# Hybrid encoder layer on one core: stick-breaking attention with rounded passes and an output added chunk by chunk, and the mixing product's second part by token tiles

## Chip, core and metric

The kernel runs on one core of a Trainium2 chip. The metric is the device time of one execution in microseconds; the time before is the median of three runs.

The engines are named as in the profile: TensorE is PE (its weight loads PEld), VectorE is DVE, ScalarE is ACT, GpSimd is POOL, SyncE is SP. SP only issues DMA here.

## What is computed

One layer (DEPTH is 1) on x of 1024 tokens by 1024 features, all in float32. A mixing sub-layer is followed by an MLP, each between two RMS norms. The mixing sub-layer has three groups that share one input projection: stick-breaking attention (4 heads of 64), a gated linear recurrence of width 512, and sliding-window attention. Their outputs are normed by group, concatenated and projected by `w_out`.

```python
u = rms_norm(h, g_pre_mix[l])
proj = jnp.einsum('bsd,de->bse', u, w_in[l])
# stick-breaking: A[t,s] = beta_ts * prod_{s<j<t}(1-beta_tj), s<t only
z = jnp.einsum('bhqd,bhkd->bhqk', qi, kf).astype(jnp.float32) * scale
log_beta = jax.nn.log_sigmoid(z)
log_1m = jnp.where(before, jax.nn.log_sigmoid(-z), 0.0)
tail = lax.cumsum(log_1m, axis=3, reverse=True) - log_1m
w = jnp.where(before, jnp.exp(log_beta + tail), 0.0)
out = jnp.einsum('bhqk,bhkd->bhqd', w.astype(vf.dtype), vf)
...
mixed = jnp.concatenate([rms_norm(o_a, ga), rms_norm(o_b, gb), rms_norm(o_c, gc)], axis=-1)
y = jnp.einsum('bse,ed->bsd', mixed, w_out[l])
h = h + rms_norm(y, g_post_mix[l])
u = rms_norm(h, g_pre_mlp[l])
f = jnp.square(jax.nn.relu(jnp.einsum('bsd,df->bsf', u, w_ff_in[l])))
y = jnp.einsum('bsf,fd->bsd', f, w_ff_out[l])
h = h + rms_norm(y, g_post_mlp[l])
```

## The kernel before

The order of each engine's work is written out by hand, and engines meet only at semaphores. A semaphore wait holds up all that is queued behind it on the same engine.

**Rounded passes.** A product of two float32 operands is done as three passes in the format fp32r: each operand is split into a rounded part (`hi`, by ScalarE) and a rest (`lo`, by VectorE), and `three_passes` multiplies hi by hi, hi by lo and lo by hi (lines 648, 650, 652). A plain float32 matmul, as the attention uses it, shows as two records in the trace and streams its columns four times.

**Stick-breaking.** 24 steps (the list `SB`): for each pair of heads (2) and each half of the queries (2), the key blocks of 128 from the last to the first, a chain of 4 or 8 steps. Keys lie on partitions, queries on columns, and the two heads side by side. The first steps of a chain are on the diagonal and have 128, 256, 384 and then 512 columns; all later ones have 512. The widths of a chain of the second half are 128, 256, 384 and five times 512. For a step s:

- TensorE makes the scores (`scores`, line 832) into PSUM banks 0 and 1 or 2 and 3, by the parity of s
- VectorE writes minus their absolute value (`minus_abs`, line 1663), ScalarE does Exp and Ln of it (lines 1233, 1234), VectorE makes the log terms `sb_l` (line 1687), and GpSimd masks the diagonal block
- VectorE adds the carry of the chain so far to the scores in PSUM (line 1697), TensorE adds the triangle product (`exponents`, line 864), and ScalarE takes the Exp: the weights (`weights_exp`, line 1213)
- TensorE sums the log terms over the block by a matrix of minus ones into two banks (`carry`, line 877), which ScalarE copies out (line 1243)
- TensorE multiplies the weights by v, accumulating over the chain (`weighted`, line 892)

TensorE's order in step s is scores(s+1), one part of the fill, exponents(s), carry(s), weighted(s-1), the other part of the fill. The fill (`FILL`) is the recurrent group's part of the output product: from step 4 on a unit of three passes ahead of the triangle, and in even steps two more behind the product with v. Four units make a bank, so 10 of its 16 banks are done in the stage, and VectorE evicts one in every second step (`recurrent_row`, line 1672). The other six follow the stage.

**Mixing product, second part.** The stick-breaking and window groups, 16 units (eight token tiles by two column halves g = 2, 3) of 12 passes. Each unit fills two banks out of a ring of four, and VectorE scales each by the group's norm and adds it to y (line 1754). All tiles of g = 2 come first, then all of g = 3, so a token tile is whole only in the second half. Then, per tile: its squares (ScalarE, line 1050), a root on VectorE of four tiny instructions (lines 1471 to 1465), the gain pass `y_gained` on GpSimd (line 639), the residual (VectorE, line 1733), h stored to DRAM, the squares of h, another root, and the scaled copy for the MLP (`normed`, line 1292).

**MLP.** Stages of seven Strassen products (P1, P2, P6, P5, P7, P3, P4) of 48 passes each. Before P1 the h of tiles 0 to 3 is transposed on TensorE (`turn_hidden_inputs(0)`, line 971) and copied to `ut` by ScalarE and VectorE in turn (lines 1300, 1774); before P2 that of tiles 4 to 7. The operands of each half product are rounded by `round_operands` (lines 1347, 1351) and `rest_operands` (lines 1798, 1805). `block_sum` makes the Strassen sums: S1 to S4 of the activations, T1 to T4 of the weights; T1 needs `wq12` and `wq11`, T2 needs `wq22`.

Of the kernel before, what the change touches and what calls it, by code (L numbers as in the profile page):

```python
# [16 lines left out]
F32 = mybir.dt.float32  # L17
# [66 lines left out]
def encoder_layer(nc, x, g_pre_mix, w_in, conv_w, conv_b, lru_wa, lru_ba, lru_wx, lru_bx,  # L84
# [5 lines left out]
    with ExitStack() as ctx:  # L90
# [16 lines left out]
        def sem(name):  # L107
# [12 lines left out]
        sb_carry = at("sb_carry", [P, 2, BANK], X_AT + 32 * K)  # L120
        neg_tri = at("neg_tri", [P, P], X_AT + 36 * K)
        neg_ones = at("neg_ones", [P, P], X_AT + 36 * K + 512)
# [10 lines left out]
        ut = at("ut", [P, 2, KD, BANK], ACT_AT + 32 * K)  # L133
        h_back = at("h_back", [P, TOK, D], ACT_AT + 32 * K)
# [6 lines left out]
        wq22 = at("wq22", [P, 4, BANK], X_AT + 16 * K)  # L141
        w_sum = at("w_sum", [P, 4, BANK], X_AT + 24 * K)
# [11 lines left out]
        y_gained = at("y_gained", [P, TOK, D], X_AT)  # L154
        out_gained = at("out_gained", [P, TOK, D], X_AT)
# [72 lines left out]
        carry_ready, carry_copied, carry_added = (  # L228
            sem("carry_ready"), sem("carry_copied"), sem("carry_added"))
        expo_ready, w_raw, w_masked, pv_done, o_copied = (  # L230
            sem("expo_ready"), sem("w_raw"), sem("w_masked"),
            sem("pv_done"), sem("o_copied"))
# [8 lines left out]
            [sem(f"h_stored{i}") for i in range(2)])  # L241
# [37 lines left out]
        TILE_SETS = ((0, 1), (2, 3), (4, 5), (6, 7))  # L279
        N_SETS = len(TILE_SETS)  # L280

# [132 lines left out]

        IN_SUMS = ("T2", "S2", "T3", "S3", "S4", "T4", "T1")
        SUMS = (IN_SUMS, ("S1", *IN_SUMS))

        def sum_count(s, name):

            if name == "T1":  # L420
                s -= 1
            if s < 0:
                return 2
            ahead = 2 + sum(len(SUMS[r % 2]) for r in range(s))
            return ahead + SUMS[s % 2].index(name) + 1
# [5 lines left out]
        def _(sp):  # L431
# [88 lines left out]
            sp.wait_ge(carry_added, adds(len(SB) - 1))  # L520
            sp.dma_start(wq11[:, :, :], block_of(0, 0, 0)).then_inc(wq_loaded[0], 16)
            for i in range(TOK):
                sp.wait_ge(h_ready, i + 1)
                sp.dma_start(h_dram[P * i:P * (i + 1), :], y[:, i, :]).then_inc(h_stored[i // 4], 16)
                if i == 3:
                    sp.dma_start(wq21[:, :, :], block_of(0, 1, 0)).then_inc(wq_loaded[2], 16)
                if i == 7:
                    sp.dma_start(wq12[:, :, :], block_of(0, 0, 1)).then_inc(wq_loaded[1], 16)
                    sp.dma_start(wq22[:, :, :], block_of(0, 1, 1)).then_inc(wq_loaded[3], 16)
# [11 lines left out]

            for half in range(2):
                sp.wait_ge(h_stored[half], 16 * 4)
            sp.wait_ge(a_lo_ready, halves(STAGES - 2, P4))
            sp.dma_start(h_back[:, :, :], h_dram.rearrange("(i p) d -> p i d", p=P))\
                .then_inc(h_loaded, 16)
# [9 lines left out]
        def _(pool):  # L556
# [48 lines left out]
            pool.wait_ge(v_turned, 2)  # L605
            after(nc.gpsimd.memset(neg_ones[:, :], -1.0))

# [29 lines left out]
            for i in range(TOK - 1):  # L637
                pool.wait_ge(y_added, banks_out(3) + 2 * (i + 1))
                nc.gpsimd.tensor_tensor(y_gained[:, i, :], y[:, i, :], rs_row[:, :], ALU.mult)\
                    .then_inc(y_gain_done, 1)  # L640
# [4 lines left out]
        def _(pe):  # L645
# [253 lines left out]
            def recurrent_out(n, ks=range(OUT_K)):  # L899
# [11 lines left out]
                elif n < N_EARLY + 4:  # L911
# [3 lines left out]
                    if bank_out(n) == 4:  # L915
                        pe.wait_ge(o_copied, 4)
# [1077 lines left out]
```

## Time and profile before

| | us |
|---|---|
| median of 3 runs (1160.93 to 1162.46) | 1162.07 |
| profiled execution | 1161.97 |
| its span | 1160.2 |
| TensorE busy | 1082.9 (93%) |
| VectorE busy | 808.4 (70%) |
| ScalarE busy | 573.5 (49%) |
| GpSimd busy | 76.1 (7%) |

How to read it: times in rows are microseconds from the start of the span. A row of the timeline has its start, its duration, the engine, the line of the kernel, the operation, what it writes and reads, and in brackets how long the engine had been idle and what ended that. The end of a matmul is modelled, so neighbouring matmuls overlap in the records. PEclk is the clock granted to TensorE as a share of its full 2.4 GHz: 1.00 is that level, 0.50 the 1.2 GHz one.

### The profile page before, as it was taken

The numbers are of one execution on the slowest core, as the hardware profiler recorded it, in microseconds if no ns is written. First come the engines' busy times: TensorE is split into PE (matmuls) and PEld (weight loads), VectorE is DVE, ScalarE is ACT, GpSimd is POOL, SyncE is SP. The second block draws the span as 40 slices with busy tenths as digits, with TensorE's granted clock in tenths as the row PEclk, the third lists the DMA queues.
The fourth block names the chain that finished last, engine by engine and source line by source line (L and its number), as shares of the span: only waits on it lengthen the run. The fifth ranks groups of instructions, "written<-read, shape, count | busy, mean of one in ns | idle before, by whom it ended". The sixth has DMA issues, their size and how long they took to land.

```text
span 1160.2 us, 12115 instructions
## 1 busy us (share of the span) xinstructions
PE 1082.9 (93%) x4844; PEld 845.5 (73%) x4844; DVE 808.4 (70%) x767; ACT 573.5 (49%) x705; POOL 76.1 (7%) x69
## 2 busy tenths in 40 slices
PE   6999999987899999838999999999999999999993
PEld 5877777876535458737888888878888878888782
DVE  2536657655454545777778777789876799867998
ACT  6313533357464640376665546653456543466353
POOL 0004113201101000400000000000000000000000
PEclk9999999978899999978999999999999999999997
DMA  7211112110000023060130310301303003016003
GB/s 220 78 45 37 37 37 73 36 38 1 1 1 1 20 102 114 37 236 1 37 109 1 109 37 21 125 1 37 109 1 114 31 19 127 1 43 248 1 1 145
DMA packets 44624, 70.44 MB, mean 61 GB/s; under 512 B 10228, under 2 KB 19736, under 8 KB 44568
## 3 DMA queue, kind: packets, MB, share of 16 engines
q1 hardware_dynamic: 43528, 69.66, 17.7%
q8 instruction: 39, 0.64, 0.2%
q10 hardware_dynamic: 1040, 0.00, 0.1%
q14 instruction: 17, 0.14, 0.0%
HBM read 61.27 MB, written 8.39 MB: 60 GB/s over the span
## 4 chain that ended last, share of the span: by engine, by line
PE 84%; DVE 8%; ACT 4%; issue 2%; DMA 1%; DVEq 0%; ACTq 0%
PE ps L648 25%; PE ps L652 25%; PE ps L650 25%; PE ps L864 2%; PE ps L724 1%; PE ps L877 1%; PE ps L787 1%; PE ps L892 1%; PE ps L832 1%; DVE sb_e L1663 1%; ACT sb_e L1233 1%; DVE out_gained L1888 1%; DMA g_pre_mix_c<-in_g_pre_mix 1%; ACT sb_w L1213 1%; DVE ps L1697 1%
## 5 line engine op out<-in xcount | busy, mean ns | idle before, releaser
L648 PE MATMUL ps<-a_op,b_op 128*128 128x512 f32 x448 | 175.9, 393 | 5.4 <-DVE b_op L1805 4.5
L648 PE MATMUL ps<-b_op,a_op 128*128 128x512 f32 x448 | 174.6, 390 | 2.7 <-issue 2.7
L650 PE MATMUL ps<-a_op,b_op 128*128 128x512 f32 x448 | 175.6, 392 | 0.0
L652 PE MATMUL ps<-a_op,b_op 128*128 128x512 f32 x448 | 175.4, 392 | 0.0
L652 PE MATMUL ps<-b_op,a_op 128*128 128x512 f32 x448 | 174.3, 389 | 0.0
L650 PE MATMUL ps<-b_op,a_op 128*128 128x512 f32 x448 | 174.3, 389 | 0.0
L648 PE MATMUL ps<-act_hi,w_hi 128*128 128x512 f32 x288 | 115.0, 399 | 3.2 <-DVE w_lo L1455 3.2
L1805 DVE TENSOR_TENSOR b_op<-wq,b_op 128x1024 fp32r<-128x1024 f32 x96 | 116.9, 1218 | 0.0
L1347 ACT CAST a_op<-f 128x1024 fp32r<-128x1024 f32 x56 | 58.8, 1049 | 116.0 <-PE ps L652 75.7
L652 PE MATMUL ps<-act_hi,w_lo 128*128 128x512 f32 x288 | 112.8, 392 | 0.0
L650 PE MATMUL ps<-act_lo,w_hi 128*128 128x512 f32 x288 | 112.6, 391 | 0.0
L648 PEld LDWEIGHTS ps<-a_op,b_op 128*128 128x128 f32 x448 | 84.9, 189 | 23.8 <-issue 6.2
L1798 DVE TENSOR_TENSOR a_op<-f,a_op 128x1024 fp32r<-128x1024 f32 x56 | 68.4, 1222 | 47.6 <-ACT a_op L1347 47.6
L1351 ACT CAST b_op<-wq 128x1024 fp32r<-128x1024 f32 x96 | 100.7, 1049 | 0.0
L648 PEld LDWEIGHTS ps<-b_op,a_op 128*128 128x128 f32 x448 | 84.1, 188 | 21.4 <-issue 4.1
L652 PEld LDWEIGHTS ps<-a_op,b_op 128*128 128x128 f32 x448 | 84.9, 190 | 17.8
L650 PEld LDWEIGHTS ps<-a_op,b_op 128*128 128x128 f32 x448 | 84.8, 189 | 17.7
L652 PEld LDWEIGHTS ps<-b_op,a_op 128*128 128x128 f32 x448 | 84.1, 188 | 17.5
L650 PEld LDWEIGHTS ps<-b_op,a_op 128*128 128x128 f32 x448 | 84.1, 188 | 17.4
L1347 ACT CAST a_op<-ut 128x1024 fp32r<-128x1024 f32 x32 | 33.7, 1052 | 76.0 <-PE ps L652 75.4
L648 PEld LDWEIGHTS ps<-act_hi,w_hi 128*128 128x128 f32 x288 | 54.4, 189 | 16.5 <-issue 5.5
L1040 ACT CAST w_hi<-stage 128x1024 fp32r<-128x1024 f32 x26 | 26.1, 1048 | 77.2 <-PE ps L652 72.0
(190 smaller groups left out, 1759.5 us busy)
## 6 DMA issues: line engine op xcount, KB each, us to landing
wq<-in_w_ff_in SPq DMA_DIRECT2D x16, 1024.0 KB, 5.3
wq<-in_w_ff_out SPq DMA_DIRECT2D x16, 1024.0 KB, 5.1
stage<-in_w_in SPq DMA_DIRECT2D x18, 512.0 KB, 4.7
y<-in_x SPq DMA_DIRECT2D x4, 1024.0 KB, 10.0
stage<-in_w_out SPq DMA_DIRECT2D x8, 512.0 KB, 3.7
h_spill<-y SPq DMA_DIRECT2D x8, 512.0 KB, 3.0
h_back<-h_spill SPq DMA_DIRECT2D x1, 4096.0 KB, 15.5
out<-y SPq DMA_DIRECT2D x8, 512.0 KB, 2.7
```

Of the source, the lines that this page charges most:

```text
L648: nc.tensor.matmul(dst, stat[0], mov[0], start=first, stop=False, skip_group_check=chained)
L650: nc.tensor.matmul(dst, stat[0], mov[1], start=False, stop=False, skip_group_check=chained)
L652: return nc.tensor.matmul(dst, stat[1], mov[0], start=False, stop=last, skip_group_check=chained)
L724: mm = nc.tensor.matmul(ps[:, 4 + 2 * m + half, :], gate_w[:, m, c, :], work[:, 0, BANK * half:BANK * (half + 1)], start=True, stop=True)
L787: mm = nc.tensor.matmul(ps[CHUNK * e:CHUNK * (e + 1), b + i // 4, P * (i % 4) + off:P * (i % 4 + 1)], qt[rows, CHUNK * c:CHUNK * (c + 1)], ...
L832: mm = nc.tensor.matmul(ps[:, 2 * (s % 2) + a, c0:], sk_t[p][rows, P * j:P * (j + 1)], sq_t[p][rows, BANK * half + c0:BANK * (half + 1)], ...
L864: mm = nc.tensor.matmul(ps[:, 2 * (s % 2) + a, c0:], neg_tri[:, :], sb_l[:, s % 2, a, c0:], start=False, stop=True, skip_group_check=True)
L1040: nc.scalar.copy(w_hi[:, slot, 1024 * s:1024 * (s + 1)], stage[:, s, :])\
L1347: nc.scalar.copy(a_op[:, half % A_SLOTS, 0], src).then_inc(a_hi_ready, 1)
L1351: nc.scalar.copy(b_op[:, (half + 3) % B_SLOTS, 0], src).then_inc(b_hi_ready, 1)
L1798: nc.vector.tensor_tensor(slot[:, 1], a_source(s, i, kk), slot[:, 0].bitcast(F32), ALU.subtract)\
L1805: nc.vector.tensor_tensor(slot[:, 1], src, slot[:, 0].bitcast(F32), ALU.subtract).then_inc(b_lo_ready, 1)
```

## The change

In the stick-breaking stage the log terms are split into `sb_hi` and `sb_lo`, and the triangle product and the sum over a block are each done in two rounded passes with tables that are exact in the rounded format. The sums of both heads go to one bank, each head's to its 64 partitions (`ones_r`). The carry is no longer added to the scores: the weights of a block are multiplied by v without it, into a bank of its own, and `add_output` multiplies the result by Exp of the carry (`sb_rest`) and adds it to the output so far.

In the mixing product's second part the units go by token tile (`OUT_ORDER`): the first two tiles of g = 2, the same two of g = 3, then both halves of each further tile. Norms are split in smaller sets and spread between the units, the first four transposes stand ahead of the last unit, T1 and T2 ahead of the operands of P2, and buffers and loads of the MLP's weights move to fit.

```diff
             def exponents(s):
                 c0 = SB[s][3]
-                masked(pe, s, log_raw, log_masked)
-                if adds(s):
-                    pe.wait_ge(carry_added, adds(s))
+                pe.wait_ge(l_lo_ready, s + 1)
                 for a in range(2):
-                    mm = nc.tensor.matmul(ps[:, 2 * (s % 2) + a, c0:], neg_tri[:, :],
-                                          sb_l[:, s % 2, a, c0:], start=False, stop=True,
-                                          skip_group_check=True)
+                    bank = ps[:, 2 * (s % 2) + a, c0:]
+                    nc.tensor.matmul(bank, tri_r[:, :], sb_hi[:, s % 2, a, c0:], start=False,
+                                     stop=False, skip_group_check=True)
+                    mm = nc.tensor.matmul(bank, tri_r[:, :], sb_lo[:, s % 2, a, c0:],
+                                          start=False, stop=True, skip_group_check=True)
                 mm.then_inc(expo_ready, 1)
...
             def carry(s):
...
-                    mm = nc.tensor.matmul(ps[:, 6 + a, c0:], neg_ones[:, :],
-                                          sb_l[:, s % 2, a, c0:], start=first_of_chain(s),
-                                          stop=True, skip_group_check=True)
+                    nc.tensor.matmul(ps[:, 6, c0:], ones_r[:, a, :], sb_hi[:, s % 2, a, c0:],
+                                     start=first_of_chain(s) and a == 0, stop=False,
+                                     skip_group_check=True)
+                    mm = nc.tensor.matmul(ps[:, 6, c0:], ones_r[:, a, :], sb_lo[:, s % 2, a, c0:],
+                                          start=False, stop=a == 1, skip_group_check=True)
...
+            for e, (s, g) in enumerate(OUT_ORDER):
+                n = 2 * TOK + 2 * e
...
+                if s == 0:
+                    pe.wait_ge(w_lo_ready, 2 * (N_IN + g + 1))
...
+                if e == len(OUT_ORDER) - 2:
+                    turn_hidden_inputs(0, range(4))
+            turn_hidden_inputs(0, range(4, KD))
...
+            act.wait_ge(tables_ready, 2)
+            nc.scalar.copy(tri_r[:, :], neg_tri[:, :]).then_inc(tables_rounded, 1)
+            nc.scalar.copy(ones_r[:, :, :], pair_ones[:, :, :]).then_inc(tables_rounded, 1)
             for s in range(len(SB)):
...
                 if s:
                     weights_exp(s - 1)
+                masked(act, s, log_raw, log_masked)
+                nc.scalar.copy(sb_hi[:, s % 2, :, c0:], sb_l[:, s % 2, :, c0:])\
+                    .then_inc(l_hi_ready, 1)
                 if not first_of_chain(s):
...
-                    nc.scalar.copy(sb_carry[:, :, c1:], ps[:, 6:8, c1:]).then_inc(carry_copied, 1)
+                    if s >= 2:
+                        act.wait_ge(o_added, s - 1)
+                    nc.scalar.activation(sb_rest[:, s % 2, c1:], ps[:, 6, c1:], ACT.Exp)\
+                        .then_inc(rest_ready, 1)
...
+            def add_output(s):
...
+                dve.wait_ge(pv_done, s + 1)
...
+                nc.vector.tensor_tensor(sb_part[:, c1:], part[:, c1:], sb_rest[:, s % 2, c1:],
+                                        ALU.mult).then_inc(part_ready, 1)
+                n_parts[0] += 1
+                dve.wait_ge(part_ready, n_parts[0])
+                nc.vector.tensor_tensor(total[:, c1:], total[:, c1:], sb_part[:, c1:], ALU.add)\
+                    .then_inc(o_added, 1)
...
-                    nc.vector.tensor_tensor(z, z, sb_carry[:, :, c1:], ALU.add)\
-                        .then_inc(carry_added, 1)
+                if s >= 2:
+                    add_output(s - 2)
                 for n in range(early(s - 1) if s else 0, early(s)):
                     recurrent_row(n)
                 if s + 1 < len(SB):
                     minus_abs(s + 1)
+                rest_log(s)
...
+            for s in range(len(SB) - 2, len(SB)):
+                add_output(s)
             left = list(range(early(len(SB) - 1), 2 * TOK))
...
+            mix_rows(0)
+            split_lo(N_IN + 3, (N_IN + 3) % 2)
+            for j in range(3):
+                for e in range(4 * j + 1, 4 * j + 5):
+                    if e == 12:
+                        mlp_root(0)
+                    mix_rows(e)
+                mix_tiles(j)
+            mix_rows(13)
+            mix_rows(14)
+            turned(0, (1, 3))
+            mix_rows(15)
+            turned(0, (5, 7))
+            rest_operands(0, [0])
+            mix_tiles(3)
+            rest_operands(0, [1])
+            mix_tiles(4)
+            mlp_root(1)
+            mlp_root(2)
+            block_sum(0, "T1")
+            mlp_root(3)
+            block_sum(0, "T2")
+            rest_operands(1, [0])
+            turned(1, (1, 3, 5, 7))
+            rest_operands(1, [1])
             block_sum(0, "S1")
-            block_sum(0, "T1")
```

ScalarE's order changes likewise: squares and roots are spread between the tiles, `round_operands(1, [0])` stands ahead of the squares of tile 7, and the load of `wq12` follows the store of tile 7's h. The load of `h_back` at the end is cut in two.

## Rows read from the trace of the kernel before

**Rows 1.** Table of stretches: start:end, length, busy time of each engine, granted clock, DMA.
```profile
279.00:430.00 151.00, 138.09 (x507) 69.26 (x508) 77.75 (x88) 83.44 (x107) 15.09 (x33) 0.97 0.05 16
560.00:1119.00 559.00, 556.28 (x2452) 459.54 (x2451) 449.80 (x339) 299.90 (x282) 0.00 (x0) 1.00 0.18 61
291.00:294.00 3.00, 1.41 (x10) 0.50 (x8) 2.01 (x2) 2.11 (x3) 0.76 (x2) 1.00 0.00 0
294.00:297.00 3.00, 2.67 (x3) 1.18 (x4) 0.50 (x2) 0.83 (x2) 0.00 (x0) 0.54 0.03 5
```

**Rows 2.** Timeline, steps 12 to 13 and 20 to 22.
```profile
350.35 0.42 DVE L1663 TENSOR_SCALAR sb_e<-ps 128x256 uint32<-128x256 uint32 x1 [0.68 <-PE ps L832]
354.78 0.69 DVE L1663 TENSOR_SCALAR sb_e<-ps 128x512 uint32<-128x512 uint32 x1 [1.99 <-PE ps L832]
...
393.03 1.23 DVE L1663 TENSOR_SCALAR sb_e<-ps 128x1024 uint32<-128x1024 uint32 x1 [1.12 <-PE ps L832]
400.26 1.21 DVE L1663 TENSOR_SCALAR sb_e<-ps 128x1024 uint32<-128x1024 uint32 x1
401.27 1.88 PE L864 MATMUL ps<-sb_l,neg_tri 128*128 128x512 f32 x4
404.79 1.08 PE L892 MATMUL ps<-sb_w,vtok 128*64 128x512 f32 x4
408.56 1.22 DVE L1663 TENSOR_SCALAR sb_e<-ps 128x1024 uint32<-128x1024 uint32 x1 [1.31 <-PE ps L832]
```

**Rows 3.** Groups by line and form, 279 to 430 us: busy, mean ns, idle before.
```profile
L1233 ACT ACTIVATE sb_e<-sb_e 128x1024 f32<-128x1024 f32 x12 | 12.7, 1057 | 33.2 <-DVE sb_e L1663 33.2
L1213 ACT ACTIVATE sb_w<-ps 128x1024 f32<-128x1024 f32 x12 | 12.1, 1011 | 9.1 <-PE ps L864 9.1
```

**Rows 4.** Timeline, mixing product's second part and MLP start.
```profile
449.90 0.75 DVE L1754 SCALAR_TENSOR_TENSOR y<-ps,rstd,y 128x512 f32<-128x512 f32 x1
...
506.21 5.19 PE L971 MATMUL ps<-ident,y 128*128 128x128 f32 x32 [14.91 <-ACT y L1292]
515.87 0.55 PE L648 MATMUL ps<-a_op,b_op 128*128 128x512 f32 x1 [4.46 <-DVE b_op L1805]
528.46 1.91 PE L971 MATMUL ps<-ident,y 128*128 128x128 f32 x16
536.62 0.77 PE L648 MATMUL ps<-a_op,b_op 128*128 128x512 f32 x1 [0.94 <-DVE ut L1774]
```

**Rows 5.** The page's costliest groups: operand rest on VectorE, rounding copy on ScalarE.
```profile
L1805 DVE TENSOR_TENSOR b_op<-wq,b_op 128x1024 fp32r<-128x1024 f32 x96 | 116.9, 1218 | 0.0
L1347 ACT CAST a_op<-f 128x1024 fp32r<-128x1024 f32 x56 | 58.8, 1049 | 116.0 <-PE ps L652 75.7
```

**Rows 6.** Timeline, end of the stick-breaking stage.
```profile
415.79 1.22 DVE L1663 TENSOR_SCALAR sb_e<-ps 128x1024 uint32<-128x1024 uint32 x1
423.64 0.75 DVE L1672 TENSOR_SCALAR y_early<-ps,rstd 128x512 f32<-128x512 f32 x1 [0.94 <-PE ps L652]
427.45 0.50 PE L648 MATMUL ps<-w_hi,f_hi 128*128 128x512 f32 x1
```

**Rows 7.** Timeline, start of the stick-breaking stage.
```profile
284.90 0.83 ACT L1233 ACTIVATE sb_e<-sb_e 128x768 f32<-128x768 f32 x1
294.09 0.41 DVE L1663 TENSOR_SCALAR sb_e<-ps 128x256 uint32<-128x256 uint32 x1
```

**Rows 8.** The page's DMA issues: a weight block, KB, us to landing.
```profile
wq<-in_w_ff_in SPq DMA_DIRECT2D x16, 1024.0 KB, 5.3
```

**Rows 9.** Timeline: a root's instruction beside a GpSimd pass, and without.
```profile
479.43 2.42 POOL L639 TENSOR_TENSOR y_gained<-y,rs_row 128x1024 f32<-128x1024 f32 x1 [0.32 <-DVE y L1754]
479.46 2.40 DVE L1462 SCALAR_TENSOR_TENSOR rs_t<-rs 128x2 f32<-128x2 f32 x1
...
498.07 0.16 DVE L1462 SCALAR_TENSOR_TENSOR rs_t<-rs 128x2 f32<-128x2 f32 x1
```

**Rows 10.** Timeline: the triangle of step 3.
```profile
294.33 3.61 PE L864 MATMUL ps<-sb_l,neg_tri 128*128 128x512 f32 x4 [1.36 <-DVE ps L1697]
```

More of the change, by code:

```diff
@@ L1288, in normed, with mix_squares @@
-            def normed(half):
-                act.wait_ge(rstd_ready, 5 if half == 0 else 7)
-                for i in range(4 * half, 4 * half + 4):
-                    act.wait_ge(h_stored[half], 16 * 4)
-                    nc.scalar.activation(y[:, i, :], y[:, i, :], ACT.Copy, scale=rstd[:, i:i + 1])\
-                        .then_inc(hn_ready, 1)
-            def turned(half):
-                for k in range(0, KD, 2):
+            def mix_squares(i):
+                act.wait_ge(y_added, mixed(i))
+                squares(i, work[:, 5, :])
@@ L1337, in b_source, with round_operands @@
                 return t[:, ks, :]
[L1339 removed]
+            def round_operands(n, kks=range(2)):
                 s, i = divmod(n, PRODUCTS)
[L1342 removed]
+                for kk in kks:
                     half = 2 * n + kk
@@ L1763, in _, with mix_tiles @@
-            rsqrt(slice(0, 4), 5)
-            dve.wait_ge(rows_loaded, 16)
-            dve.wait_ge(y_added, Y0)
-            gain_last(y_gained, rs_row[:, :])
-            norm_mix(3)
-            def turned(half):
-                for k in range(1, KD, 2):
+            def mix_tiles(j):
+                tiles = MIX_SETS[j]
+                if j in (0, 2):
+                    dve.wait_ge(xb_loaded[j // 2], 64)
+                rsqrt(slice(tiles[0], tiles[-1] + 1), rsqrt_count("mix", j))
+                for i in tiles:
+                    gained = y_gained[i // 2 % 2][:, i % 2, :]
+                    dve.wait_ge(y_gain_done, i + 1)
+                    nc.vector.scalar_tensor_tensor(
+                        out=y[:, i, :], in0=gained, scalar=rstd[:, i:i + 1],
+                        in1=x_again[:, i, :] if i < 4 else work[:, i - 4, :],
+                        op0=ALU.mult, op1=ALU.add).then_inc(h_ready, 1)
@@ new lines, in mlp_root, with mix_rows @@
+            def mlp_root(j):
+                tiles = MLP_SETS[j]
+                rsqrt(slice(tiles[0], tiles[-1] + 1), rsqrt_count("mlp", j))
+            def mix_rows(e):
+                s, g = OUT_ORDER[e]
+                cols = slice(BANK * (g % 2), BANK * (g % 2 + 1))
+                for grp in (1, 2):
+                    n = 2 * TOK + 2 * e + grp - 1
+                    dve.wait_ge(y_ready, n + 1)
+                    if grp == 2 or s >= 4:
+                        dve.wait_ge(y_added, n)
+                    if e == 0 and grp == 2:
+                        group_variance(2, 0)
+                        group_rsqrt(2)
+                    nc.vector.scalar_tensor_tensor(
+                        out=y[:, s, cols], in0=ps[:, bank_out(n), :],
+                        scalar=rstd[:, TOK * grp + s:TOK * grp + s + 1],
+                        in1=(y_early if grp == 1 and s < 4 else y)[:, s, cols],
+                        op0=ALU.mult, op1=ALU.add).then_inc(y_added, 1)
```

359 lines of the change are left out of this document (190 added, 169 removed).

## Prediction

> **What bounds the kernel now.** I read the page first, then a table of stretches, then the timeline of the two stretches that the change touches. From 560 to 1119 us TensorE is busy for 556 of 559 us [rows 1]: that body holds the bound of the whole kernel and the change leaves its products alone. The same row prices one rounded pass of 512 columns: 559 us by 2452 passes is 0.228 us. So the change can win or lose only ahead of 560 us: in the stick-breaking stage (279 to 430 us) and from the mixing product's second part to the second product of the MLP (444 to 537 us).
>
> In the stick-breaking stage TensorE is recorded busy for 138 of 151 us [rows 1], but what sets a step is a loop over three engines. From one `minus_abs` to the next a full step takes 7.23 us (393.03 to 400.26) or 8.30 us (400.26 to 408.56), in turn [rows 2]. In the second the reader sees TensorE's share: triangle and ones together from 401.27 to 404.79, the product with v, six passes of the recurrent part's product, then the scores until 408.51. In the first the chain is VectorE 1.23, Exp and Ln of 1.06 each, the weights' Exp 1.01 and the carry copy on ScalarE [rows 2, 3], then VectorE's add of the carry and a row eviction: it sums to 7.2.
>
> In the second stretch TensorE waits. Its last mixing pass ends at about 491.2; then come 14.9 us of idle before the transposes, 4.5 before product P1 at 515.87, P1 ends where the second half's transposes start, at 528.46, and P2 starts at 536.62 [rows 4]. So P1's 48 passes, partly slow, take 12.6 us and 8.2 lie between P1 and P2.
>
> **The change, part by part: stick-breaking.** All times below count from the start of a `minus_abs`.
>
> TensorE. Triangle and ones cost 3.5 us a full step now (401.27 to 404.79) [rows 2]; eight rounded passes cost 8 x 0.228 = 1.85. That is 1.7 us a full step off TensorE, some 25 us over the stage's 9,216 columns. But the new order puts something else ahead: the triangle of step s now waits for `rest_log(s)`, which VectorE does behind `minus_abs(s+1)`, which waits for the scores of s+1. Queued behind that wait on TensorE are the carry, the product with v and the next scores. So a step is: `minus_abs` 1.14 (started back to back), `rest_log` 1.22 (as the 128x1024 subtraction [rows 5]), 0.14 to be seen, passes 1.85, product with v 1.05 with its gap, recurrent passes 0 or 1.41 in turn, scores 1.25 with their gap: 6.7 or 8.1 us.
>
> VectorE. `add_output` waits for the product with v, which ends at 5.45. Its multiplication reads PSUM and costs about 0.75 (as the row of 512 at 423.64 [rows 6]), its addition about half of the 1.22 of 1024 elements [rows 5], with the waits 1.45 together. With the row eviction of 0.67, which falls into the steps without recurrent passes, the next `minus_abs` starts at 7.6. So full steps take 7.6 and 8.1, against 7.23 and 8.30: the sum of two is 0.2 us longer. TensorE's 1.7 us go into its wait. Dropped with that are the carry copy on ScalarE and the read-modify-write of PSUM; the rounding copy (1.05 [rows 5]) and a half-size Exp come in their place and have room behind it. The splits and roundings laid into steps 8, 10 and 20 fall into VectorE's 1 us of slack in the long steps: nothing; 1.5 us if that cover is gone.
>
> Narrow steps: one that follows a full step now pays the old step's addition. From 12 to 13: `rest_log(11)` until 1.65, its triangle until 2.75, the product with v 3.8, the addition 5.25, a row 5.9; in the trace it is 4.43 (350.35 to 354.78) [rows 2], +1.5. The same for 16 to 17 gives +0.8 and for the step behind each of them +0.5; the other narrow steps gain 0 to 0.5 each. With the full steps, steps 5 to 23 sum to +1.3.
>
> Start. ScalarE is full there: in the trace the Exp of step 2 starts at 284.90, `minus_abs(4)` at 294.09 [rows 7]. Two table copies add 0.5; the rounding copy stands in ScalarE's order behind the GpSimd mask, so after the Ln of step 0 ScalarE waits for 1.0, and `round_recurrent`, the squares and the next Exp are queued behind. Step by step I get the Exp of step 2 at about 288.7 and `minus_abs(4)` at 297.7: +3.6.
>
> End. From `minus_abs(23)` at 415.79 to the first pass of the remaining recurrent part at 427.45 it is 11.66 us [rows 6]. In the changed order the row of bank 9, evicted at 423.64 now, stands on VectorE behind `add_output(22)` and `(23)`. The last product with v ends at 11.6, two additions until 13.35, the row until 14.0, TensorE at 14.2: +2.5.
>
> Sum of the stage: 3.6 + 1.3 + 2.5 = +7.4. Bounds: +2 (if the start finds half its delay absorbed and the additions cost nothing) and +14.
>
> **Mixing product and MLP start.** I keep the start of the part fixed and shift it afterwards: six banks of 12 passes from 427.45 on, 444.1 [rows 6]. The upper columns are wanted at the third unit, so `split_lo(N_IN+3)` is no longer hidden: the first unit's second eviction starts at 449.90 [rows 4], ends at 450.6, the split takes until 453.0, and TensorE waits 2.0. Then 14 units of 2.72 (12 passes) and four transposes of 0.65 give the last pass at 493.9, with small waits 494.1; before it was 491.2 with one wait of 1.6. VectorE has about 3.3 of eviction and 1.6 of norm per tile in 5.4 us; four banks carry its absences of 3.3 us. I take one collision with a GpSimd gain pass (below): 2.4 us, hidden by the banks.
>
> What is won is behind the last pass. Tiles 0 to 3 are normed under the product, so their transposes need no wait. VectorE does two evictions, `turned` 5 and 7 and the first operand halves (2.4 us): P1 starts at 500.7, not 515.87, 15.2 us earlier. Of that some is given back: P1 ends at 513.3, but the second half's transposes wait for tile 7. Its h is ready at 508.0; the load of `wq12`, now issued behind it, lands 5.3 us [rows 8] and one issue later, at 514.0; T1 (2.3 us) stands ahead of `mlp_root(3)` on VectorE, ScalarE has `round_operands(1)` ahead of the squares of tile 7, so the root is done at 517.5 and tiles 6 and 7 are normed at 519.7. Then T2 and two rests (4.7) stand ahead of `turned(1)`, and P2 starts at 525.8 against 536.62. That is -10.8. T1 and T2 now sit here and no longer behind P1; nobody waits for them there. The diff leaves the end of the kernel as it was but for a load cut in two: nothing. Bounds for this part: -6 (two more collisions and a tile late) and -16 (no give-back but 5 us).
>
> VectorE's roots meet GpSimd. The root's 128x2 instruction beside a gain pass took 2.40 us, its like without one 0.16 [rows 9]: it ended as the pass ended. The sum has one such meeting at `mlp_root(0)`.
> The Trainium skill, SBUF — State Buffer, section "Who interferes with whom", says that a VectorE instruction with two SBUF inputs and a GpSimd one that reads SBUF exclude each other for a whole instruction; the trace agrees (2.40 beside 2.42 us). By it every root and norm is open to a wait for one of the eight gain passes; that is the third rival.
>
> **Sum.** The profiled execution took 1161.97 us, its span is 1160.2, so 1.8 lie around it; the median of the runs is 1162.07. 1161.97 + 7.4 - 10.8 = 1158.6, and against the median 1158.7. I forecast 1158.6.
>
> **Rivals.**
> First, TensorE binds the stick-breaking stage. For it: 138 of 151 us busy [rows 1]. Against: the 7.23 us steps have no TensorE time on their chain. If the steps in which it does bind kept their share, some 10 of the 25 us come through in place of the +1.3, with start and end (6.1) still paid: 1161.97 - 10 + 6.1 - 10.8 = 1147.3. Chance 0.13.
>
> Second, the slower side: the clock falls in the stick-breaking stage. TensorE would be busy for some 5.1 of 7.6 and 6.5 of 8.1 us. From 291 to 294 it was busy 1.41 of 3 us, and from 294 to 297 the granted clock was 0.54, nearly all at the 1.2 GHz level [rows 1]; a step's triangle took 3.61 there [rows 10] against 1.88 at 401.27 [rows 2]. So each slow stretch costs up to 1.7 us. Against it: the gaps of the new steps are under 2 us each, and the whole stage has a granted clock of 0.97 [rows 1]. With one slow stretch in two steps from step 4 on, ten, of which 1.0 us each is not hidden: 1168.6. It decides from the fourth stretch on, when the 3.4 us of gain are eaten.
> The Trainium skill, TensorE: Matmul & The Clock Gate, Part 1, says the throttled state is the default and activity releases it; the trace agrees in the rows above, and does not show a stretch as busy as the new steps. Chance 0.2.
>
> Third, collisions and VectorE's load hold up the mixing units: three more meetings of 2.4 us, of which 2 us each reach TensorE, gain 4.8: 1164.6. Chance 0.12.
>
> Fourth, the change doesn't do what it says: the rounded passes run no faster than the full ones. The 0.228 of the body speaks against it; the loop would then be 1.7 us longer in ten steps, 1175. Chance 0.03.
>
> **Chances.** The forecast (1153.5 to 1163.5) 0.5, the rivals 0.48, the rest 0.02. About 0.2% (2.3 us) is what a measurement can tell from no change. Faster: 0.31 of the forecast's 0.5, the first rival's 0.13 and 0.01: 0.45. Same: 0.16, and 0.06 of the second and third: 0.22. Slower: 0.03, 0.18, 0.08, 0.03, 0.01: 0.33. The range takes in the first rival and the clock rival: 1147 to 1170; of the forecast alone it is 1153.5 to 1163.5.
>
> **What would show it.** `minus_abs(4)` 3 to 4 us later than 294.09; full steps of 7.6 and 8.1 with a TensorE wait of 1.7 us ahead of each triangle whose releaser is `rest_log`; about 2.5 us of TensorE idle ahead of the remaining recurrent part; a wait of 2 us at the third mixing unit; P1 near 500 and P2 near 526 plus the shift; and a body of 559 us as before. Wrong it would be with a granted clock under 1.0 between 310 and 430 us, with full steps of 7 us or less, or with the first P1 pass later than 20 us behind the last mixing pass.

## Result and the profile after

The changed kernel takes 1169.8 us (median of 11 runs, 1164.4 to 1172.1) against 1161.6 (median of 11, 1160.2 to 1162.9) for the kernel before, run beside it: a ratio of 1.0067, 95% interval 1.0054 to 1.008. It is 0.7% slower. I had forecast 1158.6 and a gain. The profiled execution took 1167.29 us, its span is 1165.5: 5.3 us more than the profiled one of before.

First, where it is not lost. In the table of stretches of the changed kernel (start:end, length, busy time of PE, PEld, DVE, ACT, POOL, granted clock, DMA share, GB/s) the body is as busy as before:

```profile
280.00:310.00 30.00, 23.31 (x82) 15.28 (x83) 14.48 (x23) 17.45 (x28) 5.44 (x9) 0.56 0.00 1
310.00:350.00 40.00, 31.52 (x124) 16.03 (x124) 26.28 (x39) 23.89 (x29) 2.72 (x7) 0.96 0.00 0
350.00:390.00 40.00, 32.47 (x133) 17.81 (x133) 24.91 (x37) 20.99 (x31) 3.54 (x9) 0.91 0.00 1
390.00:428.00 38.00, 30.02 (x126) 15.54 (x125) 26.93 (x36) 24.62 (x31) 2.71 (x7) 1.00 0.09 28
545.00:1125.00 580.00, 577.29 (x2543) 477.01 (x2542) 467.55 (x351) 310.14 (x291) 0.00 (x0) 1.00 0.17 59
```

The same stretches of the kernel before:

```profile
280.00:310.00 30.00, 26.55 (x106) 15.59 (x107) 13.73 (x21) 16.76 (x28) 6.53 (x11) 0.83 0.00 1
310.00:350.00 40.00, 36.62 (x122) 16.21 (x122) 23.85 (x22) 23.46 (x25) 1.94 (x5) 1.00 0.00 0
350.00:390.00 40.00, 37.36 (x162) 20.50 (x160) 18.14 (x25) 19.92 (x31) 5.04 (x13) 1.00 0.00 1
545.00:1125.00 580.00, 577.28 (x2544) 476.75 (x2543) 469.39 (x355) 312.08 (x293) 0.00 (x0) 1.00 0.17 59
```

The reader is to see two things: 577.29 against 577.28 of 580 us in the last rows, and the clock column. In the stick-breaking stage the granted clock was 0.56, 0.96 and 0.91 where it had been 0.83, 1.00 and 1.00: TensorE has less to do (32.47 against 37.36 us of 40) and part of it is done at the 1.2 GHz level.

Then the `minus_abs` rows of the changed kernel's timeline, which answer to [rows 2, 7]; the step's length is the difference of two starts:

```profile
297.64 0.42 DVE L1733 TENSOR_SCALAR sb_e<-ps 128x256 uint32<-128x256 uint32 x1
307.38 0.68 DVE L1733 TENSOR_SCALAR sb_e<-ps 128x512 uint32<-128x512 uint32 x1
315.39 0.96 DVE L1733 TENSOR_SCALAR sb_e<-ps 128x768 uint32<-128x768 uint32 x1 [1.67 <-PE ps L872]
319.92 1.21 DVE L1733 TENSOR_SCALAR sb_e<-ps 128x1024 uint32<-128x1024 uint32 x1
...
357.43 0.42 DVE L1733 TENSOR_SCALAR sb_e<-ps 128x256 uint32<-128x256 uint32 x1 [0.59 <-PE ps L872]
363.29 0.68 DVE L1733 TENSOR_SCALAR sb_e<-ps 128x512 uint32<-128x512 uint32 x1
372.07 0.96 DVE L1733 TENSOR_SCALAR sb_e<-ps 128x768 uint32<-128x768 uint32 x1 [2.71 <-PE ps L872]
...
412.54 1.21 DVE L1733 TENSOR_SCALAR sb_e<-ps 128x1024 uint32<-128x1024 uint32 x1
420.75 1.23 DVE L1733 TENSOR_SCALAR sb_e<-ps 128x1024 uint32<-128x1024 uint32 x1 [1.21 <-PE ps L872]
428.33 1.22 DVE L1733 TENSOR_SCALAR sb_e<-ps 128x1024 uint32<-128x1024 uint32 x1
```

Steps 4 to 5, 5 to 6 and 13 to 14 take 9.74, 8.01 and 8.78 us. They are narrow steps; for the last of them I had worked out about 5.7 (5.23 before, and 0.5). The last two full steps take 8.21 and 7.58, as worked out (8.1 and 7.6).

The end of the stage and the waits after it, from the timeline of the changed kernel (answering to [rows 4, 6, 9]):

```profile
441.69 0.74 DVE L1742 TENSOR_SCALAR y_early<-ps,rstd 128x512 f32<-128x512 f32 x1
442.49 0.50 PE L688 MATMUL ps<-w_hi,f_hi 128*128 128x512 f32 x1 [2.55 <-DVE y_early L1742]
...
469.63 0.19 PEld L688 LDWEIGHTS ps<-w_hi,act_hi 128*128 128x128 f32 x1 [2.04 <-DVE w_lo L1525]
...
498.00 2.41 POOL L678 TENSOR_TENSOR y_gained<-y,rs_row 128x1024 f32<-128x1024 f32 x1 [1.05 <-DVE y L1849]
498.72 1.70 DVE L1541 TENSOR_SCALAR var<-sumsq 128x4 f32<-128x4 f32 x1 [0.81 <-ACT rs L1106]
...
511.99 2.35 POOL L678 TENSOR_TENSOR y_gained<-y,rs_row 128x1024 f32<-128x1024 f32 x1 [2.13 <-DVE y L1849]
513.14 2.28 DVE L1884 TENSOR_TENSOR a_op<-ut,a_op 128x1024 fp32r<-128x1024 f32 x1
...
516.66 0.76 PE L688 MATMUL ps<-a_op,b_op 128*128 128x512 f32 x1 [4.79 <-DVE b_op L1891]
...
529.83 2.29 DVE L1919 TENSOR_TENSOR w_sum<-wq,wq 128x2048 f32<-128x2048 f32 x1 [1.44 <-DMA wq<-in_w_ff_in]
...
541.84 0.76 PE L688 MATMUL ps<-a_op,b_op 128*128 128x512 f32 x1 [0.94 <-DVE ut L1860]
```

P2 starts at 541.84, 5.2 us later than in [rows 4], and from there on nothing differs: 5.2 of the 5.3 us. The remaining recurrent part starts at 442.49 against 427.45 in [rows 6], 15.04 later; from there to P2 it is 99.35 us where it was 109.17, so 9.8 are won back. The stage has taken 15 and was forecast to take 7.4.

### The profile page after: what moved, and what is told of

The parts are those of the page before. It is cut to its first block, busy times and chain, and to the rows that moved or that the text cites. A ratio compares the mean times of both kernels' runs of the same rounds, so it can differ in the third digit from the quotient of the medians.

```text
span 1165.5 us, 12237 instructions
## 1 busy us (share of the span) xinstructions
PE 1073.6 (92%) x4844; PEld 846.0 (73%) x4844; DVE 832.5 (71%) x838; ACT 587.5 (50%) x733; POOL 78.7 (7%) x73
## 4 chain that ended last, share of the span: by engine, by line
PE 80%; DVE 11%; ACT 4%; issue 3%; DMA 2%; SPq 1%; POOL 0%; DVEq 0%; ACTq 0%
PE ps L688 24%; PE ps L690 23%; PE ps L692 23%; PE ps L934 2%; DVE sb_lo L1749 2%; PE ps L764 1%; PE ps L902 1%; ACT swa_p L1218 1%; PE ps L872 1%; DVE sb_e L1733 1%; DVE out_gained L1974 1%; PE ps L904 1%; DMA g_pre_mix_c<-in_g_pre_mix 1%; DVE y L1927 1%; PE ps L916 1%
## 5 line engine op out<-in xcount | busy, mean ns | idle before, releaser
L1391 ACT CAST a_op<-f 128x1024 fp32r<-128x1024 f32 x56 | 58.8, 1050 | 117.3 <-PE ps L692 77.1
```

Of the source, the lines that this page charges most:

```text
L1391: nc.scalar.copy(a_op[:, (half + 2) % A_SLOTS, 0], src).then_inc(a_hi_ready, 1)
```

## The experiments

The theory after the result: the working of the steps is right, and what is missing is the slow TensorE stretches in the stick-breaking stage. Its rival: the new order itself costs more than worked out (the additions, the rests, the start), and the slow clock is hidden beside waits.

**The two parts alone.** Kernel one takes the mixing and MLP edits alone, kernel two the stick-breaking edits alone. Both are hunks of the diff shown above, with the waits on the new addition counted in the one and on the old carry in the other.

> The mixing and MLP-start part of the change alone, stick-breaking as before. My theory (the mixing part wins 11 us, the stick-breaking stage loses the rest): minus_abs times as before, third mixing unit waits 2 us, P1 at about 500.7 and P2 at about 525.5 us; span 1149 us, ratio 0.990 to 0.992. Rival (the two parts depend on each other, the gain of the mixing part is not there by itself): P2 not before 533, ratio over 0.996.

Measured: 1147.8 us, ratio 0.9883 [0.9866, 0.99]. P1 starts at 500.41 and P2 at 524.32 (I had 500.7 and 525.8). With the old stick-breaking stage the second part is worth 12.3 us at P2 and 13.5 in the medians, more than its 10.8, and the ratio is under the 0.990 to 0.992 that I expected.

> The stick-breaking part alone, mixing part as before. My theory: the stage ends 15 to 17 us later than before and all of it reaches the end: 1176 to 1181 us, ratio 1.013 to 1.017, granted clock about 0.956 to 0.961. Rival (part of the delay is absorbed by waits in the mixing part): under 1172 us.

Measured: 1179.3 us, ratio 1.0164 [1.0144, 1.0184]: 18 us lost where I had worked out 7.4. So all of the miss is in the stick-breaking part. The two parts add up to +4.5 us; the changed kernel measured +8.2, and +5.0 in a second series (below).

**Keep TensorE busy.** Six rounded passes a step are added ahead of the triangle, in the time in which TensorE waits for `rest_log`. They write a bank that the next product with v overwrites from its start; nothing reads them.

```
+            def keep_busy(s):
+                for r in range(KEEP):          # 6
+                    nc.tensor.matmul(ps[:, 4 + 3 * ((s - 1) % 2), :],
+                                     w_hi[:, (N_IN + 1) % 2, 0:P],
+                                     w_hi[:, (N_IN + 1) % 2, 0:BANK], start=True, stop=True,
+                                     skip_group_check=True)
...
+                if s:
+                    if s >= 3:
+                        pe.wait_ge(o_added, s - 2)
...
+                    keep_busy(s)
                 exponents(s)
```

> The changed kernel with six more rounded passes of 512 columns in each step, ahead of the triangle, into the bank that the next product with v overwrites; they use TensorE's idle time of 1.7 us a long step and their result is not used. Clock theory (the clock falls in the stick-breaking stage because TensorE has less to do, and costs 8 to 12 us): granted clock 1.0 in that stage from its first steps on, minus_abs(4) to (6) and (13) to (14) at 6 to 7 and 5.7 us instead of 9.7, 8.0 and 8.8, in all 1158 to 1162 us. Rival (the new order of waits alone costs it, the clock is only a sign): slow steps stay, and the passes add up to 10 us: 1170 to 1180.

Measured: 1161.4 us (11 runs), ratio 1.0003 [0.9993, 1.0012], 8.4 us under the changed kernel (4.2 under a second series of it, below): work added, time won. Its granted clock from 280 to 310, 310 to 350 and 350 to 390 us is 0.83, 1.00 and 1.00, so it still falls at the start. The three steps take 7.44, 7.25 and 6.82 us, shorter than in the changed kernel and longer than the 6 to 7 and 5.7 that I expected. Under the rival the passes could only have cost.

**Where and how many.** The same passes in steps 1 to 4 only, in steps 5 to 23 only, and three instead of six a step; beside them the changed kernel once more. The edit is shown against the kernel with six passes.

```
-                if s:
+                if s and s <= 4:      # or s > 4; the third has KEEP = 3
```

> The changed kernel with the six unused rounded passes in steps 1 to 4 only. Clock theory: the falls at the start (steps 4 to 6) cost 5 to 6 us by the trace, those later 3 us: minus_abs(6) at 311 in place of 315, 13 to 14 still slow in some runs, 1163 to 1166 us. Rival (the fall is set by the later steps): 1169 as the changed kernel.

> The same passes in steps 5 to 23 only. Clock theory: minus_abs(6) about 314 as in the changed kernel, from 315 on no slow step, all later intervals equal to those of the kernel with passes in all steps: 1163 to 1167 us. Together with the other half it should make up the 8.4 us of both.

> Three unused passes a step in place of six (0.7 us of the 1.7 us gap). If the clock falls when TensorE is idle too large a share of the time, half the passes may already hold it or not; held, it costs less in the narrow steps than six do: 1158 to 1161 us; not held, 1164 to 1170 us with slow steps left in the trace.

> The changed kernel itself once more, beside the next three on the same chip. It shows how far its time wanders by the places where the clock falls: 1164 to 1172 us, the longer the lower its granted clock. If moving the eviction of bank 9 is worth 2.5 to 4 us as worked out, this one is at 1166 to 1167 here; if it is at 1169 to 1170, that move was worth 7.

Measured: the changed kernel again 1165.6 (6 runs, 1164.1 to 1170.2), ratio 1.0051 [1.0033, 1.007], so two series of it differ by 4.2 us; start only 1162.8, 1.0017 [1.0004, 1.0031]; late only 1167.2, 1.0059 [1.0043, 1.0076]; three a step 1159.1, 0.9983 [0.9968, 0.9998]. With three passes a step the table of stretches and the steps are:

```profile
280.00:310.00 30.00, 24.11 (x112) 15.12 (x113) 17.17 (x28) 18.75 (x31) 6.20 (x11) 0.89 0.00 1
310.00:350.00 40.00, 34.35 (x142) 19.09 (x141) 29.32 (x39) 28.18 (x31) 1.95 (x5) 1.00 0.00 0
350.00:390.00 40.00, 36.37 (x173) 21.56 (x171) 24.84 (x42) 19.72 (x32) 4.69 (x13) 1.00 0.00 1
```

```profile
296.31 0.41 DVE L1749 TENSOR_SCALAR sb_e<-ps 128x256 uint32<-128x256 uint32 x1
303.76 0.68 DVE L1749 TENSOR_SCALAR sb_e<-ps 128x512 uint32<-128x512 uint32 x1
309.42 0.96 DVE L1749 TENSOR_SCALAR sb_e<-ps 128x768 uint32<-128x768 uint32 x1 [1.08 <-PE ps L873]
...
357.34 0.68 DVE L1749 TENSOR_SCALAR sb_e<-ps 128x512 uint32<-128x512 uint32 x1
363.48 0.96 DVE L1749 TENSOR_SCALAR sb_e<-ps 128x768 uint32<-128x768 uint32 x1 [1.02 <-PE ps L873]
...
420.22 1.21 DVE L1749 TENSOR_SCALAR sb_e<-ps 128x1024 uint32<-128x1024 uint32 x1
```

The three long steps are 7.45, 5.66 and 6.14 us here instead of 9.74, 8.01 and 8.78. From `minus_abs(4)` to `minus_abs(23)` it is 123.9 us, in the changed kernel 130.7, before 121.7: without the slow stretches the new steps cost 2.2 us, close to the 1.3 of the sum. The kernel before had a low clock itself in its step 4 to 5 (0.63 from 300 to 304 us); its stage in kernel one takes 120.1, and against that the new steps cost 3.8.

The start-only and late-only kernels don't bear out what I expected of them. The first has 13 to 14 at 8.78 us as in the changed kernel, and two slow steps more, at full width, of 9.16 and 8.60 us where the changed kernel has 7.58 and 7.00:

```profile
340.10 1.23 DVE L1749 TENSOR_SCALAR sb_e<-ps 128x1024 uint32<-128x1024 uint32 x1 [1.30 <-PE ps L873]
349.26 1.22 DVE L1749 TENSOR_SCALAR sb_e<-ps 128x1024 uint32<-128x1024 uint32 x1
...
404.93 1.23 DVE L1749 TENSOR_SCALAR sb_e<-ps 128x1024 uint32<-128x1024 uint32 x1 [1.44 <-PE ps L873]
413.53 1.21 DVE L1749 TENSOR_SCALAR sb_e<-ps 128x1024 uint32<-128x1024 uint32 x1
```

Its profiled execution was the slowest of its twelve (1166.4 us), so its median may have fewer of them. The second has a granted clock of 1.00 from 350 us on and still gains nothing over the changed kernel run beside it: six passes are longer than the wait in narrow steps (17 to 18 takes 6.81 us, in the changed kernel 5.66), and from `minus_abs(6)` to `minus_abs(23)` it takes 113.4 us against 112.9. Against the changed kernel beside them the start alone gains 2.8 us and the late steps alone lose 1.5; the passes in all steps gained 4.2 against that series and 8.4 against the first, so the halves don't make up the whole. I read this as the late fall costing about what six passes a step cost there; three a step repair both ends for less.

**The carry as a factor, without the rounding.** The output is still added chunk by chunk, but triangle and ones are plain float32 products again; the table copies, the copy to `sb_hi` and `rest_log` are gone.

```
-                pe.wait_ge(l_lo_ready, s + 1)
+                masked(pe, s, log_raw, log_masked)
                 for a in range(2):
...
+                    mm = nc.tensor.matmul(ps[:, 2 * (s % 2) + a, c0:], neg_tri[:, :],
+                                          sb_l[:, s % 2, a, c0:], start=False, stop=True,
+                                          skip_group_check=True)
...
-                nc.scalar.copy(sb_hi[:, s % 2, :, c0:], sb_l[:, s % 2, :, c0:])\
-                    .then_inc(l_hi_ready, 1)
...
-                rest_log(s)
```

> The changed kernel with the triangle and the sums as two plain float32 products again, without the rounding copy, the rest and the rounded tables; the carry stays a factor. Dependency theory (the rest of the log terms, queued behind minus_abs of the next step, is what made TensorE wait): full steps of 6.6 and 8.0 us in turn in place of 7.6 and 8.1, a granted clock near 1.0 from 310 us on, start less late by 3 us: 1148 to 1154 us. Rival (TensorE's 25 us matter, so giving them back costs): 1172 us or more.

Measured: 1148.0 us, ratio 0.989 [0.9876, 0.9903], 22 us under the changed kernel (18 under its second series), and the same as the mixing and MLP edits alone (1147.8). Its timeline, with full steps of 6.78 and 8.29 (others take 7.33 and 7.60):

```profile
387.77 1.22 DVE L1721 TENSOR_SCALAR sb_e<-ps 128x1024 uint32<-128x1024 uint32 x1 [1.33 <-PE ps L870]
394.55 1.22 DVE L1721 TENSOR_SCALAR sb_e<-ps 128x1024 uint32<-128x1024 uint32 x1
395.55 1.88 PE L899 MATMUL ps<-sb_l,neg_tri 128*128 128x512 f32 x4
402.84 1.22 DVE L1721 TENSOR_SCALAR sb_e<-ps 128x1024 uint32<-128x1024 uint32 x1 [1.29 <-PE ps L870]
```

The triangle starts 1.0 us behind the `minus_abs` of the next step. In the changed kernel it starts 2.4 behind (412.54, 414.94 below), and TensorE has waited for `rest_log`:

```profile
412.54 1.21 DVE L1733 TENSOR_SCALAR sb_e<-ps 128x1024 uint32<-128x1024 uint32 x1
413.67 1.21 DVE L1749 TENSOR_TENSOR sb_lo<-sb_l,sb_hi 128x1024 fp32r<-128x1024 f32 x1
414.94 0.50 PE L902 MATMUL ps<-sb_hi,tri_r 128*128 128x512 f32 x1 [1.24 <-DVE sb_lo L1749]
```

So with the carry as a factor, the whole loss is the rounding's; the rounding without the factor was not run. The rounding saves TensorE 1.7 us a full step by my sum, puts a VectorE instruction and a wait on the loop's chain and work on ScalarE at the start, and the idle time brings the slow stretches. How much is the clock's: `minus_abs(23)` starts at 428.33 us in the changed kernel, at 420.22 with three extra passes a step and at 410.17 here. So 8.1 of the 18.2 us go with the clock, and the other 10.1 stay with the clock at 1.00 from 310 us on. They are the new order and the added instructions together, which no run here prices one by one.

The carry as a factor by itself neither cost nor won anything that shows in the medians, but not because it changes nothing. With the mixing and MLP edits alone `minus_abs(23)` starts at 416.18, so here it is 6.0 us earlier; the eviction behind the additions and a slow stretch behind it give most of that back, and the third mixing unit starts 1.8 us earlier (451.56 against 453.38).

**The row ahead of the last additions.** The eviction of bank 9 is moved ahead of `add_output(22)` and `(23)`, in the changed kernel and in the one without rounding.

```
+            left = list(range(early(len(SB) - 1), 2 * TOK))
+            recurrent_row(left.pop(0))
             for s in range(len(SB) - 2, len(SB)):
                 add_output(s)
```

> The changed kernel with the eviction of bank 9 ahead of the last two output additions on VectorE. My theory of the stage's end (TensorE waits 2.6 us for that eviction, and the clock falls behind the wait): TensorE goes on without a wait, 2.5 to 4 us earlier, 1166 to 1167 us. Rival (it then waits for the additions at the second of the remaining banks): under 1 us gained, 1169.

> The variant with the carry as a factor and plain float32 products, with the same move of the eviction of bank 9. Theory as above: 1144.5 to 1146 us, beside 1148.0 without the move. Rival: no gain, 1148.

Measured: 1162.8 us (10 runs), 1.0019 [1.0005, 1.0032], and 1145.0, 0.9851 [0.9835, 0.9866]. The second is 3.0 us under its like, as worked out, and 2.8 under the mixing and MLP edits alone (1147.8): with the eviction moved, the factor does win something. The first is below the 1166 to 1167 that I expected. In it TensorE starts 13.0 us behind `minus_abs(23)` instead of 14.16 and keeps a granted clock of 1.00 behind it, and the third mixing unit starts 38.5 us behind `minus_abs(23)` instead of 41.3. That is 2.8 us, as much as its median lies under the second series of the changed kernel; under the first series it lies 7.0. Its trace has the slow steps in other places, and at full width:

```profile
353.44 1.21 DVE L1733 TENSOR_SCALAR sb_e<-ps 128x1024 uint32<-128x1024 uint32 x1
362.43 0.42 DVE L1733 TENSOR_SCALAR sb_e<-ps 128x256 uint32<-128x256 uint32 x1 [0.59 <-PE ps L872]
...
414.46 1.22 DVE L1733 TENSOR_SCALAR sb_e<-ps 128x1024 uint32<-128x1024 uint32 x1
424.26 1.23 DVE L1733 TENSOR_SCALAR sb_e<-ps 128x1024 uint32<-128x1024 uint32 x1 [1.31 <-PE ps L872]
```

That is 8.99 us for a step of 7.6 and 9.80 for one of 8.2. Which step is slow is thus not a property of the step alone.

**The rest ahead of the next absolute value.** `rest_log(s)` stands before `minus_abs(s + 1)` on VectorE, so that the triangle no longer waits behind the scores.

```
+                rest_log(s)
                 if s + 1 < len(SB):
                     minus_abs(s + 1)
-                rest_log(s)
```

> The changed kernel with the rest of the log terms ahead of minus_abs of the next step on VectorE, so that the triangle no longer waits for the next scores. Theory by my working (the three-engine loop is then VectorE's own: minus_abs, a wait for ScalarE, log terms, addition, row, rest): full steps 7.4 and 8.0 us against 7.6 and 8.2, 1166 to 1171 us, the clock still falling. Rival (this order alone is the stage's loss): full steps under 7.2, 1160 us or less.

Measured: 1164.6 us, 1.0025 [1.0015, 1.0036], a little under what I expected. The long full steps took 7.1 us (339.29 to 346.37), not 8.0, the short ones 7.4 to 7.7, and 14 to 15 took 6.0 instead of 4.5. My working of the long steps was wrong there; what remains is that the order of these two instructions doesn't settle the matter.

**A version that beats both.** The kernel without rounding and with the row first, and the fill spread evenly: one unit in each of a step's two places, in place of one and two in turn.

```
-                for _ in range(1 + slot):
-                    if slot and k == 0 or N_EARLY == FILL_BANKS:
+                for _ in range(1):
+                    if N_EARLY == FILL_BANKS:
```

> The variant of the second label (carry as a factor, plain products, eviction moved) with the recurrent part's units spread evenly, two a step in place of three and one in turn. If TensorE sets the steps with three units (8.24 us) and the VectorE loop the others (6.8 to 7.3), full steps become 7.5 each at most: 2 to 4 us less, 1141 to 1143 us. Rival (the loop over the engines sets both): 1145 as before the move.

Measured: 1139.5 us, ratio 0.9801 [0.9787, 0.9816], 22 us under the kernel before and 5.5 under its like with the uneven fill, more than the 2 to 4 that I expected. Its stretches:

```profile
310.00:350.00 40.00, 39.11 (x128) 16.74 (x127) 24.37 (x33) 21.63 (x25) 1.58 (x4) 1.00 0.00 0
350.00:390.00 40.00, 39.68 (x163) 21.19 (x164) 22.14 (x35) 20.11 (x30) 5.43 (x15) 1.00 0.00 1
390.00:428.00 38.00, 37.77 (x130) 18.99 (x128) 23.92 (x31) 18.36 (x20) 2.46 (x2) 1.00 0.27 90
```

TensorE is busy for 116.6 of 118 us and is the bound of the stage, at the full clock throughout. Full steps take 6.9 to 7.3 us, where its like has 6.8 to 8.3 and the kernel before 7.2 to 8.3. Whether the even fill would do as much with the carry added to the scores wasn't tried. Here, not in the changed kernel, cheaper products for triangle and ones would have something to give.

## Why the prediction was wrong, point by point

**The full steps: right.** 7.58 and 8.21 against 7.6 and 8.1, with TensorE waiting ahead of the triangle for `rest_log` (1.24, 1.57 and 1.30 us in the last three; I had 1.7). The first full step of each long chain took 7.0. TensorE's recorded busy time from 280 to 428 us fell by 18.8 us, part of the rest being slow, and none of it shortened the stage.

**The narrow steps: right at the full clock.** 12 to 13 took 5.86 (forecast 5.9). 13 to 14 took 8.78 (forecast about 5.7; 6.14 with three extra passes a step).

**The start: right in sum, by luck.** `minus_abs(4)` is at 297.64 (forecast 297.7). But the Exp of step 2, which I had at about 288.7, is at 286.61: ScalarE's delay was 1.7 us there and not 3.8. With three extra passes a step `minus_abs(4)` is at 296.31, so 1.3 of the 3.6 us go with the slow clock. How far this start wanders by itself: with the old stage in kernel one it is at 296.05, 2.0 later than in [rows 7].

**The end: right.** TensorE starts 14.16 us behind `minus_abs(23)` (forecast 14.2).

**Mixing and MLP start: right in sum, with one collision misplaced.** The third unit waits 2.04 us (forecast 2.0), T1 waits for the DMA of `wq12`. The mixing part starts 16.4 us later than before; against that start P1 comes 15.6 us earlier (forecast 15.2) and P2 11.2 (10.8). P1's first rest took 2.28 us beside a GpSimd gain pass that began ahead of it, against 1.22 for the like [rows 5], which is 1.1 us on P1's path; the first instruction of a root took 1.70 and nobody waited for it. I had put one collision, at `mlp_root(0)`, and none on a path.
The Trainium skill, SBUF — State Buffer, section "Who interferes with whom", has these as a lock on a port pair, with the instruction that comes second blocked; the rows agree: the root's instruction ends at 500.42 and the pass beside it at 500.41, and the rest ends 1.1 us, about its own length, behind its pass.

**The clock: the step that failed.** In the sum it is the term "steps 5 to 23 sum to +1.3", which was worked out at the full clock: from `minus_abs(4)` to `minus_abs(23)` it is 130.7 us against 121.7, +9.0. The terms beside it held (start 3.6 and end 2.5, measured as such), and the stage lost 15.0 us instead of 7.4. I had this as the second rival, with 0.2, and the sum of that rival, 1168.6, is within 1.3 us of what was measured. The clause that failed is the argument against it: "the gaps of the new steps are under 2 us each, and the whole stage has a granted clock of 0.97". The gaps are as short as I said: 1.24 to 1.57 us in the full steps, and 1.96 us at most (at 299.25) between `minus_abs(4)` and 428 us. The clock fell all the same. What TensorE did ahead of the fall at `minus_abs(13)`, in the changed kernel's table of stretches for TensorE alone (busy, granted clock, DMA):

```profile
355.00:359.00 4.00, 3.27 (x15) 1.00 0.00 0
359.00:363.00 4.00, 2.91 (x12) 1.00 0.00 0
363.00:367.00 4.00, 3.58 (x15) 0.72 0.00 0
367.00:371.00 4.00, 4.00 (x12) 0.50 0.00 0
```

It was busy for 3.27 and 2.91 of 4 us, then the clock went to the 1.2 GHz level, and in the last row TensorE is busy all the time with 12 passes. That is how a slow stretch feeds the loop: a group of four products with v takes 1.98 us at 365.92, against 1.08 for one at 416.97, and the step's chain runs through it.

The price by the traces: `minus_abs(1)` to `minus_abs(23)` takes 149.8 us in the changed kernel and 141.0 with three extra passes a step, 8.8 less. With them TensorE starts on the remaining recurrent part at 434.35 us, 6.9 later than in [rows 6], where the sum had 7.4. Another 1.4 us go behind 442.49, where TensorE had waited 2.55 us and the clock fell again (0.72 from 442.5 to 448.5 us): relative to P2's start the part is 9.8 shorter and not 11.2. The three passes don't remove this one; their kernel has the same wait of 2.55 us, and 0.75 in the 6 us behind it. 1167.3 less 10.2 is 1157.1, near the 1158.6 of the sum. The median is 2.5 us above the profiled execution, and where the slower executions lose that, no trace shows. The rival said ten stretches of 1.0 us each. Set against the kernel with three passes there are fewer and longer ones: 2.3, 2.4 and 2.6 us in the three steps and about 2.0 ahead of `minus_abs(4)`. Its mechanism held; that its sum agrees so well is in part luck.

The changed kernel also spreads more: 1164.4 to 1172.1 us, with 0.964 as the granted clock of its fastest run and 0.953 to 0.958 in the nine from 1168.0 us on; the kernel before spreads over 2.7 us. Between the two executions of it that a trace shows, the slow steps above don't explain the difference. In the profile of the second series (1164.07 us) they take 9.70, 8.05 and 8.79 us, as in the first (1167.29 us), and in kernel two's 9.73, 8.02 and 8.79. The 3.2 us between the two profiles lie behind P1: P2 starts at 541.84 and 540.56, the 10 us behind its start have a granted clock of 0.81 and 1.00, and from P2 to the end of the span it is 623.7 and 621.7 us (before: 623.6). So nearly 2 us between two profiles can come from P2's first products and from no edit.

**The other rivals.** TensorE binding the stage: not in the changed kernel (busy 117.3 of the 148 us from 280 to 428, part of it slow, against 136.1 before), but in the last experiment. Rounded passes no faster: no, the product with v starts 2.0 us behind the first of eight (414.94, 416.97). Collisions in the mixing units: the third unit's wait is the only long one there, and it is `split_lo`'s.

**What stays open.** Which stretch falls. Steps 18 to 22 keep TensorE busy for as small a share as the ones ahead of the fall (30.02 of 38 us from 390 to 428) and keep 1.00 in this execution, while the row-first kernel fell in its step 21 to 22, which starts at 414.46. With the same stick-breaking code the falls came back in the same steps in all three profiles; after an edit somewhere else in the stage they moved. No run here tells what decides it.

## What to carry to other kernels

Work taken off TensorE is worth nothing where a loop over three engines sets the step, and here it was worth less than nothing: what stood in its place was idle time at TensorE in every step, and the granted clock answered to it. When an edit turns TensorE from 92% busy to 79% in a stage, price the steps behind it at the 1.2 GHz level too, and let the higher price stand beside the forecast with equal weight. And where a change bundles ideas, price them apart: here the mixing part was worth 13.5 us, the carry as a factor nothing until the eviction was moved and about 3 then, and the rounding cost 18 to 22, about half of it with the clock held.

## What the runs showed of the hardware

Work without use sped the kernel up. Three rounded passes a step, 0.7 us of TensorE, held the granted clock at 1.00 from 310 to 390 us and made the kernel 10.7 us faster by the medians (6.5 against its second series; 8.1 by the traces at the stage's last step); six a step 8.4 (4.2).
The Trainium skill, TensorE: Matmul & The Clock Gate, Part 1, says that the throttled state is the default and that activity releases it; the runs agree, with 0.56 from 280 to 310 us in the changed kernel and 0.89 with the three passes.

The clock fell behind short gaps here: 1.96 us (at 299.25) ahead of the slow steps 4 and 5, 1.38 us (at 363.42) ahead of step 13. The slow steps are the same ones in three profiles of the same stage (4, 5 and 13), and others in nearly the same kernel (4, 5, 11 and 21 with the row first; 10, 13 and 20 with passes in steps 1 to 4), so the profile of one kernel shows their price but not their place in the next.
